# A streamed mixture of experts: down products from split parts, output stores on ScalarE's queue, expert weights in 16 KB runs

## The reference

```
gates = ...                                   # two experts per token, from a router
for e in range(16):
    he  = silu(t @ w_gate[e]) * (t @ w_up[e]) # [tokens,1024] x [1024,512]
    out = out + gates[:, e:e+1] * (he @ w_down[e])  # [tokens,512] x [512,1024]
return x + g2 * out
```

## Time and profile before

| | before |
|---|---|
| median of three executions | 894.33 us (893.77 to 894.46) |
| the profiled execution | 892.66 us, of which the span of the profile is 890.9 us |
| TensorE, weight loads, VectorE, ScalarE busy | 88%, 63%, 63%, 45% of the span |
| chain that ended last | TensorE 78%, VectorE 8%, DMA 6% |
| slots in the loop | from about 515 to 827 us |

### The profile page before, as it was taken

How to read it: one execution, slowest core, us unless ns; L and a number is a source line. 1 busy time by engine, 2 the same in 40 slices (tenths; PEclk the granted TensorE clock), 3 DMA queues, 4 the chain that set the end, 5 groups by cost and what they waited for, 6 DMA issues and landing times.

```text
span 890.9 us, 12846 instructions
## 1 busy us (share of the span) xinstructions
PE 781.9 (88%) x4072; PEld 565.0 (63%) x4073; DVE 562.2 (63%) x698; ACT 401.8 (45%) x446; POOL 80.0 (9%) x140
## 2 busy tenths in 40 slices
PE   2799999999999997489950789999999999999766
PEld 0577777878778784268830566777666677766432
DVE  1466474655647453854668586677777667777288
ACT  5225463644645363722322344555544555554303
POOL 2000211102011110220004000000000000000220
PEclk9899999999999999799995799999999999999989
DMA  8918386593947655310047978757999999997642
GB/s 320 348 67 266 88 296 176 206 271 138 349 111 278 198 185 217 120 28 1 0 145 280 374 286 309 282 194 291 367 383 380 375 379 369 384 386 280 226 175 118
DMA packets 129911, 214.85 MB, mean 241 GB/s; under 512 B 4634, under 2 KB 55898, under 8 KB 129891
## 3 DMA queue, kind: packets, MB, share of 16 engines
q1 hardware_dynamic: 127012, 204.12, 65.9%
q0 software_dynamic: 2880, 10.49, 3.0%
HBM read 186.81 MB, written 44.56 MB: 260 GB/s over the span
## 4 chain that ended last, share of the span: by engine, by line
PE 78%; DVE 8%; DMA 6%; issue 2%; POOL 2%; ACT 1%; SPq 1%; DVEq 0%; POOLq 0%; ACTq 0%
PE z L975 42%; PE fill_ps L1660 19%; PE z L1660 10%; DMA ada_w<-in_ada_w 3%; PE fill_ps L1577 2%; PE z L1076 2%; PE fill_ps L1583 1%; SPq L1200 1%; DMA slots_out<-y_slot 1%; POOL slots_in L538 1%; PE fill_ps L1104 1%; DMA exp_w<-slots_out,fetch_i 1%; DVE h_T L1425 1%; DVE v_tok L1452 1%; DVE exp_w L898 1%
## 5 line engine op out<-in xcount | busy, mean ns | idle before, releaser
L505 DVE TENSOR_TENSOR w_lo<-exp_w,w_hi 128x1024 fp32r<-128x1024 f32 x144 | 172.0, 1222 | 91.2 <-ACT w_hi L501 90.5
L501 ACT ACTIVATE w_hi<-exp_w 128x1024 fp32r (+1 forms) x144 | 151.1, 1060 | 84.1 <-PE z L975 80.2
L975 PE MATMUL z<-w_hi,x_slotT_hi 128*128 128x512 f32 x288 | 124.7, 433 | 15.2 <-DVE w_lo L505 9.3
L975 PE MATMUL z<-exp_w,hidT 128*128 x288 | 126.6, 592 | 1.2 <-DVE hidT L864 1.2
L975 PE MATMUL z<-w_hi,x_slotT_lo 128*128 128x512 f32 x288 | 116.0, 403 | 0.0
L975 PE MATMUL z<-w_lo,x_slotT_hi 128*128 128x512 f32 x288 | 115.5, 401 | 0.0
L975 PEld LDWEIGHTS z<-exp_w,hidT 128*128 128x128 f32 x288 | 54.5, 190 | 63.2 <-issue 61.7
L1660 PE MATMUL fill_ps<-h_hi,wp_hi 128*128 128x512 f32 x192 | 77.8, 405 | 1.7 <-DVE h_lo L1431 1.6
L1660 PE MATMUL fill_ps<-h_lo,wp_hi 128*128 128x512 f32 x192 | 76.6, 399 | 0.0
L1660 PE MATMUL fill_ps<-h_hi,wp_lo 128*128 128x512 f32 x192 | 76.0, 396 | 0.0
L975 PEld LDWEIGHTS z<-w_hi,x_slotT_hi 128*128 128x128 f32 x288 | 55.4, 192 | 31.8 <-DVE w_lo L505 9.7
(11 more groups left out here) (310 smaller groups left out, 1307.7 us busy)
## 6 DMA issues: line engine op xcount, KB each, us to landing
exp_w<-in_exp_w_gate SPq DMA_DIRECT2D x19, 2048.0 KB
exp_w<-in_exp_w_up SPq DMA_DIRECT2D x19, 2048.0 KB
exp_w<-in_exp_w_down SPq DMA_DIRECT2D x18, 2048.0 KB
ada_w<-in_ada_w SPq DMA_DIRECT2D x12, 2048.0 KB, 9.6
slots_in<-zeros SPq DMA_DIRECT2D x7, 2048.0 KB, 12.9
w_pair<-in_sb_w_qkv SPq DMA_DIRECT2D x24, 512.0 KB, 5.3
x_slot<-slots_in SPq DMA_DIRECT2D x18, 512.0 KB, 10.2
slots_out<-y_slot SPq DMA_DIRECT2D x17, 512.0 KB
```

The costliest lines, as they stand in the source:

```text
L501: act.activation(w_hi[:, u % RING, :].unsqueeze(1), raw_unit(b, u), ACT.Copy).then_inc(hi_ready, 1)
L505: dve.tensor_tensor(w_lo[:, u % RING, :].unsqueeze(1), raw_unit(b, u), w_hi[:, u % RING, :].bitcast(F32).unsqueeze(1), ALU.subtract).then_ ...
L975: return pe.matmul(out, lhsT, rhs, start=start, stop=stop, skip_group_check=True)
```

## The change

Five edits are made together.

1. In the loop the down products of the first three of four blocks of 128 hidden channels (KS = 3) are made from split parts, as three fp32r products each (`split_out`); the fourth stays plain float32. The down weights' three units pass through the same ring (`last_down` on ScalarE, `rest_of_down` on VectorE), so that an iteration has 11 units (WUNITS) where it had 8. The hidden rows are split as well: high part on ScalarE (`hidT_hi`), low part on VectorE. The two slots after the loop keep the plain products.
2. The high part of the next slot's rows is made by ScalarE (`next_x_hi`), not VectorE. VectorE makes the low parts of the down units ahead of its gating product and of the split of the rows, and all four next gate units behind them.
3. The weights are loaded with 16 KB of one partition contiguous in DRAM: channel p*8+k (hidden channel p*4+k) lies on partition p, where it was k*128+p (2 KB runs for gate and up, 4 KB for down). To fit, the transposes take every eighth column of `x_slot` and every fourth of `hid`.
4. The store of `y_slot` is issued by ScalarE right behind its copy, on ScalarE's DMA queue.
5. At the end three of the early additions are made by GpSimd, the first of them ahead of the late gathers; VectorE makes the low part of the second up unit behind two gated gathers instead of three, and does the second late row ahead of the last slot's output.

```
-        src = io[("exp_w_gate", "exp_w_up", "exp_w_down")[i]][0].rearrange("e (k p) f -> p e k f", p=P)
+        src = io[("exp_w_gate", "exp_w_up", "exp_w_down")[i]][0].rearrange("e (p k) f -> p e k f", p=P)
...
+        def last_down(j):
+            b = slot_expert(act, j - 1) % 2
+            act.wait_ge(exp_loaded[2], slot_fetched(act, j - 1))
+            act.wait_ge(hidT_mm, j)
+            act.activation(hidT_hi[:, :, :], fill_ps[:, 0, 0:KS * P].rearrange("p (k c) -> p k c", c=P),
+                           ACT.Copy).then_inc(hidT_hi_ready, 1)
+            for u in range(KS):
+                act.wait_ge(unit_used, units_before(j) + RING + u + 1)
+                hi_unit(act, b, 2 * RING + u)
...
         def keep_y(j):
             act.wait_ge(down_ready, j + 1)
             act.wait_ge(y_slot_stored, 16 * (j + 1))
             act.activation(y_slot[:, :], z[:, 1024:2048], ACT.Copy).then_inc(y_slot_kept, 1)
+            act.wait_ge(y_slot_kept, j + 2)
+            act.nop(nofuse=True)
+            act.dma_start(slots_out[bass.ds(j * P, P), :], y_slot[:, :]).then_inc(y_slot_stored, 16)
...
         with dve.Fori(1, m + 1) as j:
             rest_of_up(j)
-            keep_hidT(j - 1)
-            gated(j)
+            keep_split_hidT(j - 1)
+            gate_by_sig(j)
+            rest_of_down(j, range(KS))
+            keep_hid(j)
+            keep_slotT(j + 1)
+            rest_of_gate(j + 1)
...
-                mm = pe.transpose(z[:, 2048 + k * P:2048 + (k + 1) * P], src[:, k * P:(k + 1) * P], ident[:, :])
+                mm = pe.transpose(z[:, 2048 + k * P:2048 + (k + 1) * P], src[:, :].rearrange("p (c k) -> p k c", k=KD)[:, k, :],
+                                  ident[:, :])
...
+        def split_out(j):
...
+            for k in range(KS):
+                pe.wait_ge(lo_ready, units_before(j) + 2 * RING + k + 1)
+                for c in range(2):
+                    cols = slice(c * 512, c * 512 + 512)
+                    acc(zb(2 + c), hidT_hi[:, k, :], w_hi[:, k, cols], start=(k == 0))
+                    acc(zb(2 + c), hidT_hi[:, k, :], w_lo[:, k, cols])
+                    mm = acc(zb(2 + c), hidT_lo[:, k, :], w_hi[:, k, cols])
+                mm.then_inc(unit_used, 1)
+            for k in range(KS, KF):
+                for c in range(2):
+                    mm = acc(zb(2 + c), hidT[:, k, :],
+                             exp_w[:, bass.ds(b, 1), 8192 + k * D + c * 512:8192 + k * D + (c + 1) * 512], stop=(k == KF - 1))
```

More of the change, by code:

```diff
@@ L389, in build @@
     early_step = sem("early_step")
-    x_added = sem("x_added")
+    x_added = [sem(f"x_added{i}") for i in range(NT)]
     late_step = sem("late_step")
@@ L561, in phase_b_pool @@
                                     ).then_inc(gathered[t], 16)
+        for i in range(1, 3):
+            add_early(i)
     def rms(act, src, dst, done, count):
@@ L812, in keep_slotT @@
         def keep_slotT(j):
[L813 removed]
             rows_T = z[:, 2048:3072].rearrange("p (k c) -> p k c", c=P)
[L815 removed]
+            if isinstance(j, int) and j == 0:
+                dve.wait_ge(x_slotT_mm, 1)
+                dve.tensor_copy(x_slotT_hi[:, :, :], rows_T).then_inc(x_hi_ready, 1)
             dve.wait_ge(x_hi_ready, j + 1)
@@ L857, in rest_of_up, with rest_of_down, keep_split_hidT @@
             for u in us:
-                dve.wait_ge(hi_ready, (2 * RING) * j + RING + u + 1)
+                dve.wait_ge(hi_ready, units_before(j) + RING + u + 1)
                 lo_unit(dve, b, RING + u)
+        def rest_of_down(j, us):
+            b = slot_expert(dve, j - 1) % 2
+            for u in us:
+                dve.wait_ge(hi_ready, units_before(j) + 2 * RING + u + 1)
+                lo_unit(dve, b, 2 * RING + u)
+        def keep_split_hidT(j):
+            whole = fill_ps[:, 0, :].rearrange("p (k c) -> p k c", c=P)
+            dve.wait_ge(hidT_hi_ready, j + 1)
+            dve.tensor_copy(hidT[:, KS:KF, :], whole[:, KS:KF, :])
+            dve.tensor_tensor(hidT_lo[:, :, :], whole[:, 0:KS, :], hidT_hi[:, :, :].bitcast(F32),
+                              ALU.subtract).then_inc(hidT_kept, 1)
         def keep_hidT(j):
@@ L923, in phase_b_dve @@
         rest_of_up(m + 1, range(1))
-        for i in range(3):
+        for i in range(2):
             gated_y(early_y, TILES[i], 0, early_step)
-        rest_of_up(m + 1, range(1, RING))
+        rest_of_up(m + 1, range(1, 2))
+        gated_y(early_y, TILES[2], 0, early_step)
+        rest_of_up(m + 1, range(2, RING))
         gate_by_sig(m + 1)
@@ L931, in phase_b_dve @@
         keep_hidT(m + 1)
-        for i in range(NT - 1):
+        for i in range(3, NT):
             add_early(i)
-        gated_y(late_y, TILES[0], 1, late_step)
-        add_late(0)
+        for i in range(2):
+            gated_y(late_y, TILES[i], 1, late_step)
+            add_late(i)
+        dve.wait_ge(x_slot_loaded, 16 * (m + 2))
         dve.wait_ge(down_ready, m + 2)
@@ L1138, in phase_b_pe @@
             half_in(j, 1)
-            out(j - 1)
+            split_out(j)
         pe.wait_ge(x_slotT_kept, m + 2)
```

81 lines of the change are left out of this document (49 added, 32 removed).

## The result

| | before | changed |
|---|---|---|
| median | 894.39 us (893.77 to 894.53) | 882.04 us (879.72 to 883.67) |
| ratio | | 0.986 (95% interval 0.9843 to 0.9876) |
| the profiled execution | 892.66, span 890.9 | 882.33, span 880.6 |

What follows compares the result with a forecast made beforehand. TensorE's own work was taken to set the loop. Terms -15.1 + 1.5 + 0 + 0.4 - 3.4 = -16.6 took the profiled 892.66 to 876.1; with 1.67 for the median, 877.7 us, range 870.5 to 892.

Steps and rivals of the forecast that it cites:

- The products: Loop on TensorE: 18 split products and four plain halves replace sixteen plain halves, 0.95 us a slot, -15.1 in sixteen iterations.
- The parts in time: Loop: ScalarE's and VectorE's copies and units lie beside TensorE's products, cost 0; first down part 0.6 to 1.2 us early.
- the rival of ScalarE's order: Loop: ScalarE's chain runs 0.5 us past its margin in every slot, 8 us in all, 885.7; chance 0.12.
- Strides: Turns in the loop: weight loads read 32 or 16 bytes apart cost +1.5 us, lower bound 0.
- the model of 85 ns: Turns' weight loads: 85 ns halve with the clock; a stride is free while that stays below the 109 ns pace.
- a pace of 0.218: Rival, turns in the loop: strided loads double the pace, +23.5 us instead of +1.5, about 899.7; chance 0.16.
- 16 KB runs: Weight transfers in the loop: they follow the shorter period at 399 GB/s; taken 0, bounds 0 to +2 us.
- The start: Start of the loop: ScalarE's 1.02 us copy replaces VectorE's 0.69 ahead of the gate's first low part, +0.4 us.
- The end: After the loop: store, gather order and VectorE's shorter final chain together give -3.4 us (-4.9 to +1.2).
- (a): End: the last but one output's store no longer waits on SP behind a 2 MB load, -2.0 us (0 to -2.7).
- (b): End: VectorE's second up unit waits for two gathers, freeing 0.6; GpSimd's additions between gathers cost +1.0; net +0.4 us.
- (c): End: VectorE's chain after the last down product loses two additions and a gating, -1.8 us (-0.2 to -1.8).

Runs made afterwards that it cites:

- the three executions: Profiled executions of the changed kernel, unaltered: the one in the result table (median 882.04 us) and two repeats in later groups (882.02 and 881.90 us).
- no_split: Changed kernel with all down products plain again (KS = 0): 896.06 us, 1.0022 of the kernel before.
- sp_old_end: Changed kernel with the output store back on SyncE's queue and all early additions on VectorE in the order of before: 881.90 us, ratio 0.9858.
- old_end: Changed kernel with the end as before, VectorE in its old order and no additions on GpSimd: 881.72 us, ratio 0.9844.
- low_first: Changed kernel with all low parts of the last slot's up units ahead of VectorE's gated gathers at the end: 880.36 us, ratio 0.9828.

## Why the prediction was right, and where it was not

The forecast was 877.7, faster; 882.04 lies in the range. It lies 4.3 us above the forecast, near the upper end of the forecast's own 874 to 883, and the loop is not what put it there: from the third to the last turn, fifteen slots, the three executions lost 12.75 to 12.88 us, where the products and the strides give -14.2 and +1.25, -12.9. The end did.

**The products** (-15.1) held: 0.97 a slot between no_split and the changed kernel, 15.5 in sixteen, 14.0 by the medians. **The parts in time** held nearly: the first down part was the tight one, as worked out, and was late in two slots by 0.27. But its margin was smaller than the 0.6 to 1.2 given, about 0.2 (a step of 2.57 us from the copy to the next unit cost nothing, one of 2.72 cost 0.12), because this step of ScalarE's round was mis-sized: 1.16, from SP's issue of 0.36, for 2.4 to 2.9 measured. So the rival of ScalarE's order did happen, at a price of 0.55 us instead of 8.

**Strides** (+1.5) measured 1.4, which is luck: no working gave the 1.5, it was chosen between bounds. The load did grow, by 55 ns or more, and the model of 85 ns that halve with the clock and 24 of slack would have let 31 ns through; 7 came. Loads of 196 ns stand 0.112 us apart, so the listed time of a load is not what holds up the next turn; which part of it does is open. The rival, a pace of 0.218, did not happen: the pace was 0.112. So the estimate of about +23 us, for which the prediction cites the Trainium skill, "SBUF — State Buffer", Specifications, and "TensorE: Matmul & The Clock Gate", LDWEIGHTS, does not hold for these loads. **16 KB runs** (0) measured as nothing.

**The start** (+0.4) cost more: from the first to the third turn 30.25 before, 30.90 to 31.97 in the three changed executions, so +0.7 to +1.7. The steady part of it is TensorE's wait, 4.2 us for 3.3 in all three: behind the rows' high part ScalarE still has the reads of the slot table and the first gate unit ahead of the low part, and the term counted 0.4 of this 0.9. The rest is how many products ran at half clock (0.43 apart instead of 0.23), and it goes either way: the 24 products behind the wait lasted 8.59, 7.38 and 7.23 us, for 7.37 before, the 24 of slot 0 7.63, 8.54 and 7.93, for 8.10.

**The end** (-3.4) is the step that failed. Without the 0.95 of the sixteenth block the last column changed by -1.0, +1.6 and -0.6 us. Of (a), -2.0: the last but one slot's store lands after 7.99 to 8.87 us on ScalarE's queue (nine profiled executions) and after 8.43 to 9.29 on SyncE's (five, before among them); half a microsecond in the middle, and neither median nor sp_old_end shows a gain. The store's time is set by what it shares the engines with: in the two slots where no down weights are loaded it lands after 2.68 and 2.65 us on ScalarE's queue, beside a load of down weights after about 8 us and more. The 8.84 of before did not yet show this, since there the store also stood behind the load on one queue. What the prediction cited of the Trainium skill, "DMA: Bandwidth & Descriptors", Issuing engines are not separate DMA queues, that a second issuer saves the issue alone, was nearer than my row-based estimate. Of (b), +0.4: the second up unit was freed one gather earlier, but the addition that GpSimd got blocks VectorE for its whole length, which the working had as 1.0 of gatherings and not as a lock. Of (c), -1.8: VectorE's chain did shrink and TensorE's groups now follow each other closely, as was worked out, but ahead of them two late rows on VectorE hold up the copy of the last output. From the last down product to the last group's end it is 17.80, 18.47 and 16.56 us in the three executions, for 18.22 before (866.03 to 884.25) and 18.2 in old_end and sp_old_end. The 16.56 is no gain: there the down products ahead of it lasted 8.82 us for 7.13 in the first execution, at a granted clock of 0.81 for 1.00, and VectorE had caught up meanwhile.

Three slips in the working changed little. The far ends of the end add up to -5.1 and not -4.9, so the forecast's own range starts at 874.5. A contiguous element on VectorE costs 1.15 ns by the working's own fixed part, not 1.0. And 0.95 in sixteen slots is 15.2, not 15.1.

In sum, by the traces of the three executions: ahead of the loop 0 to +2.7, start +0.7 to +1.7, fifteen slots -12.8, and behind the last turn +0.7 to -2.0, with the sixteenth slot in it. That is -9.3 to -13.7 in all; the median's -12.3 lies among these.

## What to carry to other kernels

A change of five edits may owe all of its gain to one: undo each by itself, and compare what the traces show in every slot (the period) before medians that scatter by 2 us. Before an operation is moved to an idle engine, look for what the two engines share and what the move does to the engine's whole round: 0.35 us of issue became 1.8 us or more on ScalarE, and an addition on GpSimd made an operation of VectorE 2.7 times as long. A stop that has one cause by the table of waits may have a second behind it, which shows only once the first is removed.

## What the runs showed of the hardware

A float32 low part of 128 x 1024 on VectorE, with both operands in SBUF (1.22 us), took 3.28 beside an addition of GpSimd of 3.40. That addition took 2.34 where VectorE was idle when it began (the first execution), 3.40 where it began beside a gated gather. In low_first a product of VectorE with one operand in PSUM (`hid`) took its usual 0.68 in the middle of such an addition.

A weight load of 128 columns took 196 to 206 ns with elements 32 or 16 bytes apart, and 139 to 141 contiguous, yet moved the pace of transposes from 0.109 to 0.112 us (32 bytes) and from 0.110 to 0.117 (16 bytes) only.

A DMA issued on ScalarE's queue, listed with 0.35 us, put 1.8 to 2.3 us between the operations around it, more than half of it work that had run beside the copy when SyncE issued the store. A read of a small table took 0.64 us for 0.28 when SyncE read the same table at that time.

A store of 0.5 MB on ScalarE's queue took 2.65 us without a load beside it, 6.8 to 7.2 beside loads in 2 and 4 KB runs, and 10.5 to 13.1 beside loads in 16 KB runs.
